# Order of VectorE's and ScalarE's steps around the last sigmoid gate of a hybrid decoder layer

## What is computed

```python
x = x + hier_moe(rmsnorm(x, g_ffn), ...)                 # the stage before
e = rmsnorm(p @ w_ple_proj, g_ple)                       # computed long before, kept in eT
x = x + sigmoid(rmsnorm(x, g_ple_gate) @ w_ple_gate) * e # the gate: 1024 x 1024 weights
y = rmsnorm(x, g_final)                                  # the output rows
```

## Time and profile before

| | us |
|---|---|
| median of three runs | 1096.93 |
| the profiled execution | 1097.6 |
| its span (first to last instruction) | 1095.8 |
| TensorE matmul busy in the span | 953.8 |
| VectorE busy | 599.1 |
| ScalarE busy | 411.7 |
| mean granted TensorE clock | 0.922 of full speed |

### The profile page before, as it was taken

The page is one execution under the profiler, slowest core; times in us unless marked ns, Lnnn a source line. Parts: engine busy times, 40 slices in busy tenths (PEclk is TensorE's granted clock), DMA queues, the critical chain, the costliest instruction groups (busy, mean ns, idle before and its releaser), DMA issues.

```text
span 1095.8 us, 16848 instructions
## 1 busy us (share of the span) xinstructions
PE 953.8 (87%) x5389; PEld 699.4 (64%) x5389; DVE 599.1 (55%) x1069; ACT 411.7 (38%) x687; POOL 172.1 (16%) x214
## 2 busy tenths in 40 slices
PE   5597888978889788897886999998999999999874
PEld 3486776867778576686765999775444444443553
DVE  3675875758757587575875654263333342432424
ACT  3454562635636456264564432153111111111312
POOL 0043241232412324123240000010000000000000
PEclk9798998979889899898996999988999999999988
DMA  7171351813617136171361850591999999999001
GB/s 185 40 180 45 103 156 38 215 43 95 164 38 212 46 93 166 38 212 46 95 179 45 230 167 25 177 370 39 351 394 384 384 389 392 378 390 333 0 1 43
DMA packets 208599, 188.51 MB, mean 172 GB/s; under 512 B 8000, under 2 KB 166392, under 8 KB 208568
## 3 DMA queue, kind: packets, MB, share of 16 engines
q1 hardware_dynamic: 207352, 187.12, 53.3%
q10 hardware_dynamic: 1216, 0.98, 0.3%
HBM read 176.88 MB, written 11.21 MB: 172 GB/s over the span
## 4 chain that ended last, share of the span: by engine, by line
PE 64%; DVE 16%; ACT 9%; issue 7%; DMA 1%; DVEq 1%; ACTq 0%; SPq 0%
PE bank L1685 11%; PE bank L1389 6%; PE bank L1713 5%; PE bank L1390 5%; PE bank L1641 5%; PE bank L1391 5%; PE bank L1549 4%; PE bank L1648 3%; PE bank L1464 3%; PE bank L1578 3%; PE bank L1733 3%; DVE wlo L961 2%; PE bank L1553 2%; DVE ii L1092 2%; ACT whi L699 2%
## 5 line engine op out<-in xcount | busy, mean ns | idle before, releaser
L1389 PE MATMUL bank<-h_hi,whi 128*128 128x288 f32 x640 | 212.0, 331 | 28.2 <-DVE wlo L961 28.1
L1390 PE MATMUL bank<-h_lo,whi 128*128 128x288 f32 x640 | 202.9, 317 | 0.0
L1391 PE MATMUL bank<-h_hi,wlo 128*128 128x288 f32 x640 | 201.8, 315 | 0.0
L1389 PEld LDWEIGHTS bank<-h_hi,whi 128*128 128x128 f32 x640 | 134.4, 210 | 47.3 <-DVE wlo L961 33.6
L1390 PEld LDWEIGHTS bank<-h_lo,whi 128*128 128x128 f32 x640 | 134.3, 210 | 0.5
L1391 PEld LDWEIGHTS bank<-h_hi,wlo 128*128 128x128 f32 x640 | 133.9, 209 | 0.0
L1284 DVE TENSOR_TENSOR xT<-xT,bank 128x288 f32<-128x288 f32 x128 | 49.5, 450 | 152.4 <-PE bank L1648 152.4
L699 ACT ACTIVATE whi<-wb 128x1024 fp32r<-128x1024 f32 x82 | 86.8, 1060 | 95.6 <-PE bank L1391 92.1
L961 DVE TENSOR_TENSOR wlo<-wb,whi 128x1024 fp32r<-128x1024 f32 x82 | 103.4, 1262 | 20.2 <-ACT whi L699 12.4
L887 ACT ACTIVATE Gs<-bank 128x512 f32<-128x512 f32 x16 | 9.6, 597 | 145.1 <-PE bank L1685 145.1
L1641 PE MATMUL bank<-pick,htok 96*128 96x256 f32 x240 | 59.0, 387 | 1.1 <-ACT yb L866 1.1
(11 more groups left out here) (349 smaller groups left out, 1632.8 us busy)
## 6 DMA issues: line engine op xcount, KB each, us to landing
wb<-in_w SPq DMA_DIRECT2D x80, 1024.0 KB, 8.6
wb<-in_w_in SPq DMA_DIRECT2D x80, 512.0 KB, 4.0
wb3a<-in_w SPq DMA_DIRECT2D x16, 1024.0 KB, 8.6
arena<-in_state_ssd SPq DMA_DIRECT2D x16, 512.0 KB, 5.6
out_new_ssd_s<-arena SPq DMA_DIRECT2D x16, 512.0 KB, 5.8
wb<-in_w_br_ssd SPq DMA_DIRECT2D x16, 512.0 KB, 3.9
wb<-in_w_br_lru SPq DMA_DIRECT2D x8, 512.0 KB, 3.8
wb<-in_w_out SPq DMA_DIRECT2D x8, 512.0 KB, 5.0
```

Of the source, the lines that this page charges most:

```text
L1389: mm(bP[i % 2][:, 0:T], hi, h_hi[:, k, :], start=(k == 0), stop=False)
L1390: mm(bP[i % 2][:, 0:T], hi, h_lo[:, k, :], start=False, stop=False)
L1391: ins = mm(bP[i % 2][:, 0:T], lo, h_hi[:, k, :], start=False, stop=(k == KC - 1))
```

## The change

VectorE's order for each j becomes gate_out(j-1), gate_sum(j-1), gate_in(j), in place of gate_in(j), gate_out(j-1), gate_sum(j-2). On ScalarE the square of block j-1 comes ahead of the sigmoid of block j, and the sigmoid's wait for x4_(j-2) goes, since the order implies it. The lists of step names follow. No instruction is added or removed, and TensorE's program stays as it is.

```diff
         act_end = Steps(sem("act_end"), [f"sg{j}" for j in X3] + ["grs"]
-                        + ["sig0"] + [n for j in range(1, 8) for n in (f"sig{j}", f"sy{j - 1}")] + ["sy7", "yrt", "out0", "out2", "out4"])
+                        + ["sig0"] + [n for j in range(1, 8) for n in (f"sy{j - 1}", f"sig{j}")] + ["sy7", "yrt", "out0", "out2", "out4"])
         dve_end = Steps(sem("dve_end"), [n for p in range(4) for n in (f"x3_{p}", f"x3_{p + 4}", f"hg{p}", f"hg{p + 4}")] + ["t0"]
-                        + [n for j in range(1, 8) for n in (f"t{j}", f"x4_{j - 1}", f"xg{j - 1}", f"acc{j - 2}") if n != "acc-1"]
-                        + ["x4_7", "xg7", "acc6", "acc7", "yrs", "out1", "out3", "out5"])
+                        + [n for j in range(1, 8) for n in (f"x4_{j - 1}", f"xg{j - 1}", f"acc{j - 1}", f"t{j}")]
+                        + ["x4_7", "xg7", "acc7", "yrs", "out1", "out3", "out5"])
...
             for j in range(8):
-                act.wait_ge(dve_end.sem, dve_end.at(f"t{j}"))
-                if j >= 2:
-                    act.wait_ge(dve_end.sem, dve_end.at(f"x4_{j - 2}"))
-                ch.step(act_f(sg[j % 2], gt[j % 2], ACT.Sigmoid), act_end, f"sig{j}")
                 if j >= 1:
                     square_x4(j - 1)
+                act.wait_ge(dve_end.sem, dve_end.at(f"t{j}"))
+                ch.step(act_f(sg[j % 2], gt[j % 2], ACT.Sigmoid), act_end, f"sig{j}")
             square_x4(7)
...
             for j in range(8):
-                gate_in(j)
                 if j >= 1:
                     gate_out(j - 1)
-                if j >= 2:
-                    gate_sum(j - 2)
+                    gate_sum(j - 1)
+                gate_in(j)
             gate_out(7)
-            gate_sum(6)
             gate_sum(7)
```

## The result

The changed kernel takes 1082.40 us in the median of four runs (1081.85 to 1083.69), against 1096.95 for the kernel before beside it. The ratio is 0.9872 with a 95% interval of 0.9854 to 0.9889: about 14 us faster, 1.3% (the two medians differ by 14.55). The profiled execution took 1081.85 us, with a span of 1080.0.

The account below looks back on a forecast made before the run. In the tail, TensorE's in-order waits for VectorE's xg blocks were taken to bound the kernel. Saving 12.46 through gate 7 plus 1.6 after gave 14.06, 1097.6 to 1083.5 profiled; median put at 1083.2, range 1081.2 to 1085.8.

Parts of the forecast that it names:

- The mechanism: Tail: TensorE waits for xg_(j-1), which VectorE queues behind t(j); 2.00 us idle per period would go.
- The period: TensorE becomes the bound: 3.88 for a gate plus 0.39 for transposes, 4.27 us against 6.43 before.
- The low stretch in gate(4): Low TensorE clock after the 2.00 us idle, 1.66 us in all, taken as gone with that idle.
- Rival 1: A low-clock stretch stays or falls anew among the gates though TensorE has no gap: 1084.9 us, chance 0.20.
- The end: After gate 7, VectorE owes only block 7's chain; last sum starts 3.2 to 3.35 us behind, saving 1.6.
- The table load: ScalarE's square-root load after the last square, done at +4.15, hidden by 0.3 us behind the sum ending about +4.5.
- The sum by terms: Saving of 12.46 us from gate(2)'s end to gate 7's end, plus 1.6 after it: 14.06.
- Slack: Room beside gate(j+1) on TensorE: 1.1 us for VectorE to be free for t(j+1), 1.3 for xg.
- rival 3: VectorE and ScalarE's alternation loop, adding up to 3.2 us, takes 6.4 and keeps the period: 1095.3 us, chance 0.02.
- the margin: Median put at 1083.2 us, above the 1082.9 that follows if the runs' median stays 0.67 below the profiled execution.
- gate(2)'s start and low stretch: Gate(2) still begins at 1043.63 and ends at 1049.22, its low stretch kept because the 3.48 us idle remains.

Follow-up runs that it names:

- first gap filled: Changed kernel with eleven idle-time matmuls on TensorE behind gate(1) only, in its 3.48 us wait for xg_0: 1082.15 us, ratio 0.9860.
- transposes later, early loads: Changed kernel with TensorE's output transposes one block later and two one-element activations loading ScalarE's tables early: 1076.94 us, ratio 0.9808.

## Why the prediction was right

The forecast was 1083.2 with a range of 1081.2 to 1085.8; the median is 1082.40.

- **The mechanism**, xg_(j-1) queued behind t(j) on VectorE with TensorE in order behind it, holds: moving that one step gives the whole ratio, ScalarE's half nothing, and an edit on TensorE that avoids the same wait gives the same period.
- **The period**: forecast 4.27, measured 4.21. The mis-sized term is the transposes: I took the 0.39 of a set that starts on an idle TensorE; between two gates they take 0.33. Five periods make that 0.3.
- **The low stretch in gate(4)** went, as forecast. The Trainium skill's page "TensorE: Matmul & The Clock Gate", section "Why this matters for your kernels", names only gaps longer than these as lowering the clock. The runs show that shorter ones can: under the same 2.00 us idle the stretch comes back in other gates, and it stays away when the idle is filled. Rival 1 did not come about.
- **The end**: the last sum was to start 3.2 to 3.35 after gate 7 and started at 1072.48, 3.29 after 1069.19. The table load was the next in line, as worked out, and since TensorE was at full clock there (0.76 for the sum, not 1.22) the load ended last: the root starts 4.22 after gate 7, against 6.16 before. That is 0.3 more than the 1.6 of the sum, the most that the table load was to leave. This 0.3 is luck: the prediction put the last sum at the low clock, and the profiles do not show that the change decides it. Two kernels with the same end (first gap filled; transposes later, early loads) have it at the low clock, 1.20, and their root starts 4.6 after gate 7, near the 4.5 at which the sum was forecast to end.
- **The sum by terms**: forecast 12.46 + 1.6 = 14.06; measured 33.81 - 21.06 = 12.75 up to gate 7's end (1048.13 to 1069.19), 1.94 behind it, 14.7 in all. The rest of the difference between the two profiled executions lies ahead of the tail.
- **Slack**: forecast 1.1 us a period for VectorE; the idle ahead of t is 1.06, and the kernels with more work, 0.82 and 2.05 us, lie on either side of the switch as they should. In the changed kernel with the transposes later, VectorE for some blocks does not wait for TensorE, and its t then start 3.18 apart (1045.86, 1049.04, 1052.22): this is the loop that rival 3 added up to 3.2. One slack was misread: that of xg was put at 1.3 and is 1.6 (ya at 1054.53, taking 0.37 and 0.04 of handover, the transposes that read it at 1056.55), as the transposes of the block before lie ahead of the gate as well. Nothing in the sum rested on it.
- **The median** came out 0.8 under the forecast, of which 0.6 is the two terms above and 0.3 the margin by which the forecast stood above its own sum, 1082.9. What is left, 0.1, is less than what runs differ by (1081.85 to 1083.69).

What the prediction took as given, that gate(2)'s start and low stretch are fixed, was right for this change only. It was TensorE's own order that held them: 3.2 us of idle (3.48 less 0.30) and 1.6 of clock (5.59 less 3.95).

## What to carry to other kernels

Where an in-order engine waits for a result, look at what its producer has queued ahead of it: a finished block behind a step that needs the consumer's next output costs the consumer a stall in each period, and moving the older block ahead cost nothing here. Then look at the consumer's order too: deferring its use of the result by one block does the same without touching the producer, and here it also removed a stall that the producer's order could not reach. After such a move name the slack that the new order rests on (1.06 us here, 1.3 for work that can also fill the wait for the square): 0.82 us more work in each block was hidden among the gates and cost 0.5 only at the end, while of 2.05 us the part beyond the slack was paid in every period.

## What the runs showed of the hardware

TensorE, at full clock before, went to the low clock after an idle of 3.48 us ahead of gate(2) in all nine profiles that have this idle. After idles of 2.00 us it did so for some only: for one of the five between gate(2) and gate(7) in each of three profiles, each time in another gate. It did not after the idles of 0.66 us between the gates in two profiles, nor after the one of 1.88 us and the one of 1.03 us ahead of gate(2), each seen in one profile. Each low stretch cost 1.6 to 1.7 us. The three transposes of a block (128, 128 and 32 tokens) took 0.33 us of TensorE between two sets of matmuls and 0.39 at the head of a set behind idle. A table load of ScalarE took 1.28 us and the one-element activation behind it 0.20.
